# Attention row blocks of 64 queries for two heads on one NeuronCore, with small softmax values and half sums in PSUM

## The reference

```python
s = einsum('bnqhgd,bnkhd->bhgnqk', qc, kb) * (HEAD_DIM ** -0.5)   # 64 queries x 192 keys
s = where(valid, s, -1e30)
m = maximum(max(s, axis=-1, keepdims=True), sink)
p = exp(s - m)
denom = sum(p, axis=-1, keepdims=True) + exp(sink - m)
o = einsum('bhgnqk,bnkhd->bnqhgd', p / denom, vb)
...
a = (a * silu(za)) @ w_att_out
```

## Time and profile before

| | |
|---|---|
| median of three runs | 1160.34 us |
| the profiled execution | 1160.82 us |
| its span in the trace | 1159.0 us |
| PE busy | 1057.2 us, 91% |
| DVE busy | 600.9 us, 52% |
| ACT busy | 456.7 us, 39% |
| POOL busy | 504.0 us, 43% |
| first scores of attention | 135.72 us |
| last product with the values ends | 308.11 us |

### The profile page before, as it was taken

The page is one execution under the profiler, slowest core; times in us unless marked ns, Lnnn a source line. Parts: engine busy times, 40 slices in busy tenths (PEclk is TensorE's granted clock), DMA queues, the critical chain, the costliest instruction groups (busy, mean ns, idle before and its releaser), DMA issues.

```text
span 1159.0 us, 12193 instructions
## 1 busy us (share of the span) xinstructions
PE 1057.2 (91%) x4977; PEld 871.6 (75%) x4977; DVE 600.9 (52%) x817; ACT 456.7 (39%) x778; POOL 504.0 (43%) x226
## 2 busy tenths in 40 slices
PE   6899997888999999999998975699899999999996
PEld 5677775777778788878898864577688888888885
DVE  2664266888754782364667899753712312312422
ACT  5134455666753433443226733234321221221232
POOL 3124342444534454434743465416353453453452
PEclk9999998999999999999999987799999999999998
DMA  6222221211243224322221311122232332332321
GB/s 211 71 73 74 73 73 37 73 37 61 85 147 108 73 73 158 117 73 100 83 82 46 92 55 54 42 67 73 73 109 73 109 109 73 109 109 73 109 73 73
DMA packets 92312, 98.65 MB, mean 85 GB/s; under 512 B 3250, under 2 KB 87888, under 8 KB 92256
## 3 DMA queue, kind: packets, MB, share of 16 engines
q1 hardware_dynamic: 92256, 97.88, 26.2%
HBM read 95.77 MB, written 2.10 MB: 84 GB/s over the span
## 4 chain that ended last, share of the span: by engine, by line
PE 64%; DVE 23%; ACT 9%; issue 2%; POOL 1%; DMA 0%; DVEq 0%; SPq 0%; POOLq 0%; ACTq 0%
PE ps L312 57%; ACT P L597 5%; DVE Fm L1027 4%; DVE sm L583 2%; DVE sm L586 2%; DVE Fm L1150 1%; PE ps L574 1%; PE ps L762 1%; ACT whi L241 1%; DVE tmp L397 1%; DVE tmp L1360 1%; DVE sm L585 1%; DVE M L419 1%; POOL P L916 1%; PE ps L576 1%
## 5 line engine op out<-in xcount | busy, mean ns | idle before, releaser
L243 POOL TENSOR_TENSOR wlo<-raw,whi 128x1024 fp32r<-128x1024 f32 x168 | 413.5, 2464 | 604.4 <-ACT whi L241 604.3
L312 PE MATMUL ps<-Hh,whi 128*128 128x512 f32 x848 | 346.0, 408 | 26.0 <-ACT whi L241 11.2
L312 PE MATMUL ps<-Hl,whi 128*128 128x512 f32 x848 | 337.4, 398 | 0.0
L241 ACT ACTIVATE whi<-raw 128x1024 fp32r<-128x1024 f32 x168 | 175.3, 1048 | 103.4 <-PE ps L312 97.6
L312 PE MATMUL ps<-Hh,wlo 128*128 128x512 f32 x848 | 213.8, 391 | 0.0
L312 PEld LDWEIGHTS ps<-Hh,whi 128*128 128x128 f32 x848 | 163.6, 193 | 66.7 <-issue 16.1
L312 PE MATMUL ps<-Ah,whi 128*128 128x512 f32 (+1 forms) x576 | 200.0, 370 | 10.9 <-ACT whi L241 9.2
L312 PE MATMUL ps<-Al,whi 128*128 128x512 f32 (+1 forms) x576 | 196.2, 363 | 0.0
L312 PEld LDWEIGHTS ps<-Hl,whi 128*128 128x128 f32 x848 | 163.8, 193 | 35.6 <-issue 2.4
L312 PEld LDWEIGHTS ps<-Hh,wlo 128*128 128x128 f32 x848 | 161.1, 190 | 34.1
L312 PEld LDWEIGHTS ps<-Ah,whi 128*128 128x128 f32 x576 | 104.3, 190 | 32.3 <-ACT whi L241 11.6
(11 more groups left out here) (269 smaller groups left out, 1005.3 us busy)
## 6 DMA issues: line engine op xcount, KB each, us to landing
raw<-in_w_in SPq DMA_DIRECT2D x35, 1024.0 KB, 5.3
raw<-in_w_up SPq DMA_DIRECT2D x16, 1024.0 KB, 5.3
raw<-in_w_down SPq DMA_DIRECT2D x16, 1024.0 KB, 5.0
raw<-in_w_att_out SPq DMA_DIRECT2D x4, 1024.0 KB, 5.0
raw<-in_w_sg_out SPq DMA_DIRECT2D x4, 1024.0 KB, 5.1
raw<-in_w_o SPq DMA_DIRECT2D x4, 1024.0 KB, 5.0
raw<-in_w_out SPq DMA_DIRECT2D x3, 1024.0 KB, 5.1
Fm<-in_x SPq DMA_DIRECT2D x2, 1024.0 KB, 6.6
```

Of the source, the lines that this page charges most:

```text
L241: eh = A(lambda e, s=s, src=src, kk=kk: e.activation(wtile(whi, s, kk), src, ACT.Copy), raw_ev[b], used)
L243: lo_ev.append(G(lambda e, s=s, src=src, kk=kk: e.tensor_tensor(wtile(wlo, s, kk), src, f(wtile(whi, s, kk)), ALU.subtract), eh))
L312: return e.matmul(ps[:, bk, 0:c1 - c0], wt, x[:, k, c0:c1], start=st, stop=sp)
```

## The change

A row block keeps 128 rows, but they are 64 queries of two heads (the even and the odd head of a pair) in place of 128 queries of one. The two blocks t = 0, 1 of a pair take the first and the second 64 queries of the group of 128. All 128 rows of a block then see the same 192 keys.

- The split queries are written in another order (`q_at`), so that 64 queries of two heads stand side by side as 128 weight columns.
- The score matmuls have 192 columns (64 or 128 for p = 0), and there are still 8 of them. Bank 4 and bank 5 each hold two blocks of 192 columns.
- One instruction takes the row maxima for p > 0, and 4 exponentials of 128 partitions take the place of 8 of 64.
- The sinks are spread by two new copies before the rounds (`sinks4`).
- Maximum, maximum with the sink, sink term and denominator lie in free columns of bank 5 of PSUM. The negative maximum, the row sums and the reciprocal stay in SBUF.
- The half sums go back into PSUM bank 3 and not into SBUF, the upper half first.
- `at_norm(i)` stands at the end of round i, no longer at the start of round i+1. Banks 4 and 5 come free with the reciprocal and not with the last exponential.

```diff
-            c = 64 + 24 * (i % 2)
-            return [sm[:, c + 4 * n:c + 4 * n + 4] for n in range(5)]
+            c = 400 + 16 * (i % 2)
+            mx, m, es, den = [ps[:, 5, c + 4 * n:c + 4 * n + 4].rearrange("p (b t) -> p b t", b=2) for n in range(4)]
+            c = 80 + 12 * (i % 2)
+            ng, rs, rd = [sm[:, c + 4 * n:c + 4 * n + 4].rearrange("p (b t) -> p b t", b=2) for n in range(3)]
+            return mx, m, es, den, ng, rs, rd
...
+            for b in range(2):
+                for t in range(2):
+                    _, k0, W = span_of(p, t)
+                    out = ps[:, 4 + b, 192 * t:192 * t + W]
+                    c = 1024 * j + 128 * (2 * p + t)
+                    lhs = qs[b][:, c:c + 128]
...
+            else:
+                e1 = V(lambda e: e.tensor_reduce(mx, s_b, AX.X, ALU.max), ev)
...
-            for h in range(4):
-                for o, c0, c1 in reach(p):
-                    e5 = A(lambda e, h=h, o=o, c0=c0, c1=c1: e.activation(
-                        Pf[o:o + 64, u, h, c0:c1], s_b[o:o + 64, h, c0:c1], ACT.Exp, bias=ng[o:o + 64, h:h + 1],
-                        scale=0.125, accum_out=rs[o:o + 64, h:h + 1]), st[("m", i)], e0,
-                        p_free[u])
-            bank_free[4] = bank_free[5] = e5
+            for b in range(2):
+                for t in range(2):
+                    c0, _, W = span_of(p, t)
+                    e5 = A(lambda e, b=b, t=t, c0=c0, W=W: e.activation(
+                        Pf[:, u, b, t, c0:c0 + W], s_b[:, b, t, 0:W], ACT.Exp, bias=ng[:, b, t:t + 1], scale=0.125,
+                        accum_out=rs[:, b, t:t + 1]), st[("m", i)], e0, p_free[u])
...
+            e7 = V(lambda e: e.tensor_tensor(den, rs, es, ALU.add), st[("e", i)])
+            e8 = V(lambda e: e.reciprocal(rd, den), e7)
+            bank_free[4] = bank_free[5] = e8
...
-                    tmp[64 * b:64 * b + 64, s, x], ps[0:64, 3, x], tmp[0:64, s, x], ALU.add), ea))
-            bank_free[3] = half_sum[1]
+                    ps[64 * b:64 * b + 64, 3, x], ps[0:64, 3, x], tmp[0:64, s, x], ALU.add), ea))
+            release(s, half_sum[1])
...
+            bank_free[3] = ev
...
             for i in range(19):
-                if 1 <= i < 17:
-                    at_norm(i - 1)
                 if i < 16:
                     at_scores(i)
...
                     at_exp(i)
+                    at_norm(i)
```

More of the change, by code:

```diff
@@ L460, in build, with q_at @@
         q_ev = {}
-        qs = (A8h, A8l)
+        qs = (Ah[:, 0:4096], Al[:, 0:4096])
+        def q_at(b):
+            return qs[b].rearrange("p (j n e c) -> p j n e c", j=4, n=8, e=2)
         def q_done(k):
+            j, e2 = k // 2, k % 2
             def done(s, er):
@@ L469, in done @@
                 for b in range(2):
[L470 to L473, removed]
+                    o, x, y = 64 * b, 64 - 64 * b, q_at(b)[:, j, :, e2]
+                    src = tmp[o:o + 64, s, 0:512].rearrange("p (n c) -> p n c", n=8)
+                    ea = A(lambda e, y=y, o=o, src=src: e.activation(y[o:o + 64], src, ACT.Copy), er)
+                    q_ev[k].append(V(lambda e, y=y, o=o, x=x, src=src: e.tensor_tensor(
+                        y[x:x + 64], src, f(y[o:o + 64]), ALU.subtract), ea))
                 release(s, q_ev[k][1])
@@ L547, in before, with span_of @@
             return evs[(what, i)] if i >= 0 else None
-        Pf = P[:].rearrange("p (u h n) -> p u h n", u=2, h=4)
-        s_b = ps[:, 4:6, :].rearrange("p b n -> p (b n)").rearrange("p (h n) -> p h n", h=4)
+        Pf = P[:].rearrange("p (u b t n) -> p u b t n", u=2, b=2, t=2)
+        s_b = ps[:, 4:6, 0:384].rearrange("p b (t n) -> p b t n", t=2)
         p_free = [None, None]
         st = {}
-        reach = lambda p: ((0, 0, 64), (64, 0, 128)) if p == 0 else ((0, 0, 192), (64, 64, 256))
         e_p0 = V(lambda e: e.memset(P[:], 0.0), got["meta"], e_ss[-1])
-        def at_small(i):
-            c = 64 + 24 * (i % 2)
-            return [sm[:, c + 4 * n:c + 4 * n + 4] for n in range(5)]
+        sinks4 = sm[:, 64:80].rearrange("p (j b t) -> p j b t", j=4, b=2)
+        by_head = sinkb.rearrange("p (j e b o) -> p j e b o", j=4, e=2, b=2)
+        for o in range(2):
+            src = by_head[64 * o:64 * o + 64, :, o].broadcast_to([64, 4, 2, 2])
+            e_sk = V(lambda e, o=o, src=src: e.tensor_copy(sinks4[64 * o:64 * o + 64], src), e_sink)
+        def span_of(p, t):
+            return (0, 0, 64 + 64 * t) if p == 0 else (64 * t, 128 * (p - 1) + 64 * t, 192)
+        def at_small(i):
+            c = 400 + 16 * (i % 2)
[3 more added lines that the diff above has]
+            return mx, m, es, den, ng, rs, rd
         def at_scores(i):
@@ L566, in at_scores @@
             g = j // 2
[L567 to L577, removed]
@@ L578, in at_scores @@
-            mx, ng, es, _, _ = at_small(i)
-            sk = sinkb[:, 4 * j:4 * j + 4].rearrange("p (e b) -> p b e", b=2)
-            v4 = lambda a: a.rearrange("p (b e) -> p b e", b=2)
-            for o, c0, c1 in reach(p):
-                e1 = V(lambda e, o=o, c0=c0, c1=c1: e.tensor_reduce(mx[o:o + 64], s_b[o:o + 64, :, c0:c1], AX.X,
-                                                                   ALU.max), ev, before(st, "den", i - 2))
-            e2_ = V(lambda e: e.scalar_tensor_tensor(v4(mx), v4(mx), 0.125, sk, ALU.mult, ALU.max), e1, e_sink)
@@ L586, in at_scores @@
-            V(lambda e: e.tensor_scalar(ng, mx, -1.0, None, ALU.mult), e2_)
-            st[("m", i)] = V(lambda e: e.tensor_tensor(v4(es), sk, v4(mx), ALU.subtract), e2_)
+            for b in range(2):
[4 more added lines that the diff above has]
+                    lhs = qs[b][:, c:c + 128]
+                    ready = (bank_free[4], bank_free[5], *q_ev[2 * j], *q_ev[2 * j + 1], *k_ev)
+                    T(lambda e, out=out, lhs=lhs, k0=k0, W=W: e.matmul(out, lhs, kdh[:, g, k0:k0 + W], start=True,
+                                                                       stop=False), *ready, signal=False)
+                    ev = T(lambda e, out=out, lhs=lhs, k0=k0, W=W: e.matmul(
+                        out, lhs, kdl[:, g, k0:k0 + W], start=False, stop=True), signal=(b == 1 and t == 1))
@@ new lines, in at_scores @@
+            mx, m, es, _, ng, _, _ = at_small(i)
+            sk = sinks4[:, j]
+            if p == 0:
+                for t in range(2):
+                    e1 = V(lambda e, t=t: e.tensor_reduce(mx[:, :, t], s_b[:, :, t, 0:64 + 64 * t], AX.X, ALU.max), ev)
+            else:
+                e1 = V(lambda e: e.tensor_reduce(mx, s_b, AX.X, ALU.max), ev)
+            e2_ = V(lambda e: e.scalar_tensor_tensor(m, mx, 0.125, sk, ALU.mult, ALU.max), e1, e_sk)
+            V(lambda e: e.tensor_scalar(ng, m, -1.0, None, ALU.mult), e2_)
@@ L589, in at_exp @@
+            st[("m", i)] = V(lambda e: e.tensor_tensor(es, sk, m, ALU.subtract), e2_)
         def at_exp(i):
             p, u = i // 4, i % 2
-            _, ng, es, rs, _ = at_small(i)
+            _, _, es, _, ng, rs, _ = at_small(i)
             e0 = e_p0
             if i in (4, 5):
-                e0 = V(lambda e: e.memset(Pf[64:128, u, :, 0:64], 0.0), p_free[u])
-            for h in range(4):
-                for o, c0, c1 in reach(p):
-                    e5 = A(lambda e, h=h, o=o, c0=c0, c1=c1: e.activation(
-                        Pf[o:o + 64, u, h, c0:c1], s_b[o:o + 64, h, c0:c1], ACT.Exp, bias=ng[o:o + 64, h:h + 1],
-                        scale=0.125, accum_out=rs[o:o + 64, h:h + 1]), st[("m", i)], e0,
-                        p_free[u])
@@ L601, in at_exp @@
-            bank_free[4] = bank_free[5] = e5
+                e0 = V(lambda e: e.memset(Pf[:, u, :, 1, 0:64], 0.0), p_free[u])
+            for b in range(2):
+                for t in range(2):
+                    c0, _, W = span_of(p, t)
+                    e5 = A(lambda e, b=b, t=t, c0=c0, W=W: e.activation(
+                        Pf[:, u, b, t, c0:c0 + W], s_b[:, b, t, 0:W], ACT.Exp, bias=ng[:, b, t:t + 1], scale=0.125,
+                        accum_out=rs[:, b, t:t + 1]), st[("m", i)], e0, p_free[u])
@@ L605, in at_norm @@
             u, W = i % 2, 128 if i < 4 else 256
[L606 to L611, removed]
+            _, _, es, den, _, rs, rd = at_small(i)
+            e7 = V(lambda e: e.tensor_tensor(den, rs, es, ALU.add), st[("e", i)])
+            e8 = V(lambda e: e.reciprocal(rd, den), e7)
+            bank_free[4] = bank_free[5] = e8
+            rb = rd.rearrange("p b (t o) -> p b t o", o=1).broadcast_to([128, 2, 2, W])
+            st[("p", i)] = G(lambda e: e.tensor_tensor(Pf[:, u, :, :, 0:W], Pf[:, u, :, :, 0:W], rb, ALU.mult), e8)
         def at_turn(i):
@@ L618, in at_turn @@
                     ev = T(lambda e, k=k, h=h: e.transpose(ps[:, 6 + k, 128 * h:128 * h + 128],
-                                                           Pf[:, u, h, 128 * k:128 * k + 128], ident[:]),
```

(14 more changed lines are left out.)

## The result

The changed kernel takes 1126.88 us (median of 4 runs, 1124.23 to 1126.95) against 1160.66 us of the kernel before beside it. The ratio is 0.9703, with a 95% interval of 0.9687 to 0.9720. The forecast was 1129 us, 1125 to 1138.

What follows compares the result with a forecast made beforehand. In attention PE waited for a softmax chain over three engines, 9.86 us a round against 8.3 of its own work. Savings of 30.6 and 1.1 us sum to 31.7, from 1160.82 to 1129 us, range 1125 to 1138.

Steps and rivals of the forecast that it cites:

- PE sets the round: Middle attention rounds: banks come free at about 7.0 us, PE reaches the next scores at 8.3; chance 0.75, 1129 us.
- Small values in PSUM: Small DVE softmax instructions with values in PSUM: 0.16 to 0.2 us each, bounds below 0.15 and 1.82.
- the slower one: Rival: small DVE instructions writing or rereading PSUM cost 1.8 us each, 1196 us; chance of slower or none 0.04.
- Exponentials: On ACT, four of 128 partitions replace eight of 64, at 0.53 us each, ending at 6.2 us of the round.
- The rival with exponentials at double price: 128-partition exponentials cost what two on 64 do, so the softmax chain still ends last: 1145 us; chance 0.09 (1135 to 1145).
- Normalization and weight tile on POOL: The moved normalization runs 7.0 to 8.9 us, the weight tile's low part 8.9 to 11.3; nothing waits.
- 192 columns: Eight score matmuls of 192 columns instead of 256 on PE: 0.11 us apart, 0.9 us for eight.
- The half-rate rival: Narrow score matmuls stream at half rate, 0.16 us each: 0.4 us lost in 12 rounds, 1134 us; chance 0.07.
- The 82 ns of the prediction: Score matmul price of 192 / 2.4 + 2.5 from the skill; would lower the sum some 3 us; not adopted.
- The sum: Attention stage: 30.6 us saved in rounds 0 to 15 and 1.1 in round 16, 31.7 us in all.
- The clock: PE's clock taken as full speed, 1.00 of 2.4 GHz; a clock below that in the stage counted as wrong.
- Freeing the port would be worth nothing by itself: Rival: line 586 in PSUM still waits for POOL, exponentials start at 4.1 us all the same: 1129 us; chance 0.05.

Runs made afterwards that it cites:

- e5: The changed kernel with each exponential of 128 partitions cut into two of 64, lower and upper half in turn: 1140.84 us, ratio 0.9826.
- e6: The changed kernel with eight exponentials of 64 partitions, all four of the lower half first, then the upper four: 1130.75 us, ratio 0.9739.
- e3: The changed kernel with the normalization of a block moved back to the start of the next round: 1124.58 us, ratio 0.9691.
- e7: The kernel before with one edit, the normalization at the end of its own round: 1157.43 us, ratio 0.9980.
- e1: The changed kernel with small softmax values and half sums back in SBUF, blocks and place of normalization kept: 1128.40 us, ratio 0.9728.
- e2: The kernel before, blocks of 128 queries kept, with maximum, sink term, denominator and half sums in PSUM: 1138.61 us, ratio 0.9814.
- e4: The changed kernel with each exponential issued a second time into memory that nothing reads: 1132.04 us, ratio 0.9749.

## Why the prediction was right

**PE sets the round: right.** 8.16 us measured, 8.27 worked out. The step of 7.37 from the earlier trace rows held to 0.1.

**Row maxima: right.** One instruction of 0.97 us.

**Small values in PSUM: right.** 0.16 to 0.17 us with results in PSUM, at the cheap end of the range that went from 0.15 to 1.82. The rival in which they cost 1.8 us, the slower one, had no sign of itself.

**Start of the exponentials: right.** Worked out at 4.1 behind the copy of the transposes, measured 3.81.

**Exponentials: right in kind, too dear.** 0.53 each was carried over from the kernel before, 0.40 came. There the halves took turns (e5 against e6); with 128 partitions there is no turn. So the banks came free at 6.0 and not at 7.0: some 0.5 us by the exponentials, 0.3 by their earlier start and 0.2 by the small instructions behind them. For the middle rounds this made no difference, since PE sets them. The rival with exponentials at double price fell: on 128 partitions they start 0.40 apart, as on 64 (e6).

**Normalization and weight tile on POOL: right.** They ran from 6.1 to 10.3 us of the round (worked out: 7.0 to 11.3), and PE never waited for a weight tile in the middle rounds. The move itself is neutral with the change (e3) and worth some 3 us without it (e7).

**192 columns: right.** The matmuls start 0.11 us apart. The half-rate rival fell, and so did the rate by columns alone. The 82 ns of the prediction were no price for this stream: the section of the Trainium skill that it names, "Back-to-back issue gap" of "TensorE: Matmul & The Clock Gate", gives that formula for a single matmul by itself and says that at few columns it counts too little.

**The sum: 31.7 worked out, 33.8 measured.** Of the missing 2.1 us, 0.8 is round 0: put at 7.2 and measured at 6.39, PE's own floor. Its chain is shorter by the cheaper exponentials too: its banks come free at 6.18. 0.1 in each of the nine later rounds makes another 1.0, 0.1 to 0.15 in each of rounds 1 to 3 some 0.4 more, and 0.1 in each of rounds 16 and 17 another 0.2. Rounds 4 and 5 went the other way, 7.42 and 7.53 for 7.37: there the banks came free just in time, 0.06 us ahead of the next scores, as forecast.

**The clock: read in one place only.** The prediction took 1.00 from rounds 7 to 14. In rounds 1 and 5 the kernel before ran at 0.80 and 0.82. The sum did not suffer, since it adds up the new rounds from rows at full clock and subtracts them from the measured stretch. But waiting was not all that it saved: some 4 us were clock.

**"Freeing the port would be worth nothing by itself": wrong in two rounds, right in the others.** That step looked only at the negative maximum and only at a middle round. e1 shows that the maximum with the sink, which has two inputs in SBUF, meets the weight tile. In round 5 the clearing of P makes the exponentials depend on DVE, so the delay comes out on PE, and round 6 is longer by the clock. And without the blocks the port is the larger part of what was to be had (e2, 22.0 us).

## What to carry to other kernels

A stage that waits on a chain over three engines can be freed from several sides, and the gains do not add: here 32 us (blocks and queue order) and 22 us (PSUM) make 34 together, since PE's own 8.2 us a round is the end for each. Work out that floor first, from a stretch where the engine doesn't wait, and the rest of the sum is a question of whether each link stays under it. And look at what small DVE instructions meet on POOL: on 4 numbers a partition they took up to 2.1 us beside a busy POOL where all inputs lay in SBUF, two of them (602, 585) or one (586), and 0.16 to 0.17 beside it with an input in PSUM.

## What the runs showed of the hardware that was not expected

Exponentials with row sums on ACT overlap with the next one when both use the same partitions: 0.40 us apart on 128 as on 64 partitions, 0.53 when the instruction goes from partitions 0 to 63 to 64 to 127 or back. The reading of the row sum shows it: the next exponential starts 0.09 us after the start of that reading, or only 0.02 after its end.

An idle time of PE of 1.94 us in e1, and two of 1.61 and 1.60 us in rounds in a row in e4, were followed by a stretch at a granted clock of 0.50, the 1.2 GHz level (180.1 to 183.4 and 181.1 to 184.4 us). There a delay in one round cost nearly as much again in the next, some 1.6 us. Not every idle time did that: 1.35 us in each middle round left the kernel before at 1.00. In the changed kernel the stage has no such idle time and the clock stays at 1.00.
